# Cached values loaded 128 partitions wide, small buffers moved apart, attention scores over 64 partitions with the two heads of a pair side by side

## What is computed

```python
def _attend(q, k, v, mask, sinks):
    scores = jnp.einsum('...qkgd,...skd->...kgqs', q, k).astype(jnp.float32) * (HEAD_DIM ** -0.5)
    scores = jnp.where(mask, scores, NEG_INF)
    sink = jnp.broadcast_to(sinks.reshape(N_KV, GROUP, 1, 1).astype(jnp.float32), scores.shape[:-1] + (1,))
    probs = jax.nn.softmax(jnp.concatenate([scores, sink], axis=-1), axis=-1)[..., :-1]
    return jnp.einsum('...kgqs,...skd->...qkgd', probs.astype(v.dtype), v)
...
def sample_window_attention(q, k, v, sinks, k_buf, v_buf):
    B, T = q.shape[:2]
    kk = jnp.concatenate([k_buf.astype(k.dtype), k], axis=1)
    vv = jnp.concatenate([v_buf.astype(v.dtype), v], axis=1)
```

## Time and profile before

| what | value |
|---|---|
| device time, median of 3 runs | 1117.38 us |
| lowest and highest of the 3 | 1115.88 and 1118.61 us |
| span of the profiled execution | 1115.6 us |
| PE busy | 936.1 us (84%) |
| DVE busy | 403.5 us (36%) |
| ACT busy | 267.6 us (24%) |
| POOL busy | 120.9 us (11%) |
| moved by DMA | 268.84 MB, mean 241 GB/s |

### The profile page before, as it was taken

The page is one execution under the profiler, slowest core; times in us unless marked ns, Lnnn a source line. Parts: engine busy times, 40 slices in busy tenths (PEclk is TensorE's granted clock), DMA queues, the critical chain, the costliest instruction groups (busy, mean ns, idle before and its releaser), DMA issues.

```text
span 1115.6 us, 14382 instructions
## 1 busy us (share of the span) xinstructions
PE 936.1 (84%) x5619; PEld 631.1 (57%) x5619; DVE 403.5 (36%) x874; ACT 267.6 (24%) x508; POOL 120.9 (11%) x195
## 2 busy tenths in 40 slices
PE   7999952999999999999927998888887887887844
PEld 6999952888999998978823333322222222222311
DVE  4765831776564545265561111010110011001126
ACT  3556430444344342311110111100110011011111
POOL 3000401000000000000012122011111111110003
PEclk8999985999999999999957999999999999989986
DMA  9233440211122142723494899999999999999962
GB/s 290 76 77 76 127 96 21 75 42 52 62 77 76 55 135 77 195 100 137 176 416 179 336 422 420 422 421 424 422 422 421 423 424 423 420 422 423 422 243 112
DMA packets 87896, 268.84 MB, mean 241 GB/s; under 512 B 32657, under 2 KB 59405, under 8 KB 67330
## 3 DMA queue, kind: packets, MB, share of 16 engines
q1 hardware_dynamic: 77602, 254.89, 58.8%
q0 software_dynamic: 10240, 13.21, 3.6%
HBM read 263.17 MB, written 15.16 MB: 249 GB/s over the span
## 4 chain that ended last, share of the span: by engine, by line
PE 50%; DMA 27%; DVE 10%; SPq 4%; another core or an unknown queue 3%; ACT 3%; issue 2%; POOLq 0%; POOL 0%; DVEq 0%; ACTq 0%
DMA slot<-in_w_up 26%; PE ps L764 25%; PE ps L1066 7%; PE ps L1093 5%; PE ps L981 5%; SPq L459 4%; PE ps L851 2%; PE ps L805 1%; PE ps L885 1%; DVE rawL L1450 1%; PE ps L875 1%; DVE hL L1536 1%; PE ps L1049 1%; PE ps L1001 1%
## 5 line engine op out<-in xcount | busy, mean ns | idle before, releaser
L1066 PE MATMUL ps<-slot,xt 128*64 128x512 f32 x512 | 248.3, 634 | 71.5 <-DMA slot<-in_w_up 70.5
L1067 PE MATMUL ps<-slot,xt 128*64 128x512 f32 x512 | 248.6, 635 | 0.0
L1066 PEld LDWEIGHTS ps<-slot,xt 128*64 128x64 f32 x512 | 69.3, 144 | 222.1 <-issue 152.8
L764 PE MATMUL ps<-xTh,wh 128*128 128x260 f32 x704 | 149.4, 294 | 1.5 <-DVE rawL L1450 1.5
L764 PE MATMUL ps<-xTl,wh 128*128 128x260 f32 x704 | 144.0, 287 | 0.0
L764 PE MATMUL ps<-xTh,rawL 128*128 128x260 f32 x704 | 144.0, 286 | 0.0
L1928 DVE COPY xt<-ps 128x512 f32<-128x512 f32 x32 | 22.1, 692 | 295.8 <-PE ps L1049 295.8
L1093 PE MATMUL ps<-slot,hT 128*64 128x512 f32 x512 | 116.9, 598 | 1.4 <-DVE hT L1938 1.4
L764 PEld LDWEIGHTS ps<-xTh,wh 128*128 128x128 f32 x704 | 112.4, 194 | 2.8 <-issue 1.8
L764 PEld LDWEIGHTS ps<-xTl,wh 128*128 128x128 f32 x704 | 111.5, 194 | 0.0
L764 PEld LDWEIGHTS ps<-xTh,rawL 128*128 128x128 f32 x704 | 110.9, 193 | 0.0
(11 more groups left out here) (314 smaller groups left out, 1210.2 us busy)
## 6 DMA issues: line engine op xcount, KB each, us to landing
slot<-in_w_down SPq DMA_DIRECT2D x32, 2048.0 KB, 28.7
slot<-in_w_gate SPq DMA_DIRECT2D x64, 1024.0 KB, 27.8
slot<-in_w_up SPq DMA_DIRECT2D x64, 1024.0 KB, 32.4
raw<-in_w_in SPq DMA_DIRECT2D x18, 1024.0 KB, 5.1
raw<-in_w_in SPq DMA_DIRECT2D x16, 256.0 KB, 4.5
raw<-in_w_lru_out SPq DMA_DIRECT2D x4, 1024.0 KB, 5.1
raw<-in_w_attn_out SPq DMA_DIRECT2D x16, 256.0 KB, 4.6
wo_raw<-in_w_o SPq DMA_DIRECT2D x4, 1024.0 KB, 8.6
```

The lines of the kernel that those rows point to most:

```text
L764: last = mm(out_of[:, a, 0:HT], w[:, k, :], x[:, k, a * HT:(a + 1) * HT], start=(k == 0 and n == 0), stop=(k == KT - 1 and n == 2))
L1066: mm(out[0:CAP, :], tokens, w[:, q, :], start=start, stop=stop)
L1067: last = mm(out[CAP:P, :], tokens, w[:, 4 + q, :], start=start, stop=stop)
```

## The change

The zero-padded `kz` becomes `kT`, in which the two key heads of a pair lie in partitions 0 to 63 and 64 to 127 without zeros. A score product runs over 64 partitions. Half of a unit (`hh`) is now two query heads of each of the pair's two key heads, and the program alternates between the lower and the upper 64 partitions, with results in different PSUM banks. The softmax pieces `sk8` and `es` and the copies into `pT` are addressed to suit. ACT writes `kT` in one instruction instead of two, DVE copies the new key into `kS` in 2 instructions instead of 4, and POOL's two memsets go.

`cV` is loaded with all 128 partitions, and the new value is written over partition 0 afterwards by a DMA that waits for the load and is issued behind the nine outputs. `kwin` and `snew` move to the end of the region of `kT` and `vtok`, so the copies into `pT` no longer wait for them; SP waits for the outputs instead, before it loads `lnG` over that region.

```diff
@@ -163,8 +163,8 @@
...
-        kz = at("kz", [P, 2, 2, T], F32, oE)
-        vtok = at("vtok", [P, NB, 256], F32, oE + 4 * KB2)
+        kT = at("kT", [P, 2, T], F32, oE)
+        vtok = at("vtok", [P, NB, 256], F32, oE + 2 * KB2)
...
@@ -177,8 +177,8 @@
...
-        kwin = at("kwin", [P, 256], F32, oI + 12288)
-        snew = at("snew", [NS, 512], F32, oI + 13312)
+        kwin = at("kwin", [P, 256], F32, oE + 8288)
+        snew = at("snew", [NS, 512], F32, oE + 9312)
...
@@ -471,6 +471,7 @@
...
+            sp.wait_ge(s_kv_out, 64)
...
@@ -597,12 +598,6 @@
...
-            pool.wait_ge(s_cst, 6)
-            gp.memset(kz[0:HD, :, 1, :], 0.0).then_inc(s_cst, 1)
-            pool.wait_ge(s_cst, 7)
-            gp.memset(kz[HD:P, :, 0, :], 0.0).then_inc(s_cst, 1)
-            pool.wait_ge(s_cst, 8)
-
...
@@ -624,14 +619,15 @@
             pool.wait_ge(s_cv, 8)
             pool.wait_ge(s_ocT, 1)
             pool.dma_start(cK[:, :, :], A["cache_k"].rearrange("b w k d -> w b (k d)")).then_inc(s_ck, 16)
-            pool.dma_start(cV[1:P, :, :], A["cache_v"][:, 1:WIN, :, :].rearrange("b w k d -> w b (k d)")).then_inc(s_cv_ld, 16)
-
-            pool.dma_start(cV[0:1, :, :], snew[:, 256:512]).then_inc(s_cv_ld, 16)
+            pool.dma_start(cV[:, :, :], A["cache_v"].rearrange("b w k d -> w b (k d)")).then_inc(s_cv_ld, 16)
 
             pool.wait_ge(s_ocv, 2)
             pool.dma_start(O["conv_prompt"][0, :, :], oc[0:3, :]).then_inc(s_oc_out, 16)
             for b in range(NS):
                 pool.dma_start(O["conv_sample"][b, :, :], oc[4 + 4 * b:7 + 4 * b, :]).then_inc(s_oc_out, 16)
+
+            pool.wait_ge(s_cv_ld, 16)
+            pool.dma_start(cV[0:1, :, :], snew[:, 256:512]).then_inc(s_cv_ld, 16)
 
             pool.wait_ge(s_oc_out, 16 * 9)
             gp.memset(qz[:, :, :], 0.0).then_inc(s_qz, 1)
@@ -847,22 +843,24 @@
...
                 lo = 0 if n else P
-                for h in range(GRP):
-                    last = mm(pair[2][:, h // 2, (h % 2) * 256 + lo:(h % 2) * 256 + 256], qT[:, 4 * p2 + h, n * P:(n + 1) * P],
-                              kz[:, p2, par, (n - 1) * P + lo:(n + 1) * P], start=True, stop=True)
+                for h2 in range(2):
+                    for par in range(2):
+                        half = slice(par * HD, (par + 1) * HD)
+                        last = mm(pair[2][:, par, h2 * 256 + lo:h2 * 256 + 256], qT[half, 4 * p2 + 2 * hh + h2, n * P:(n + 1) * P],
+                                  kT[half, p2, (n - 1) * P + lo:(n + 1) * P], start=True, stop=True)
                 last.then_inc(s_sc, 1)
 
-            def probs_t(u, par):
+            def probs_t(u, hh):
                 p2, n = _UNITS[u]
...
@@ -901,7 +899,7 @@
...
-                pe.wait_ge(s_skd, 6)
+                pe.wait_ge(s_skd, 4)
...
@@ -1177,11 +1175,7 @@
                     sc.activation(xp[:, i, 3 + HT:3 + SEQ], ps[:, 1, 0:SEQ - HT], ACT.Identity, bias=bias)
                     sc.activation(xp[:, i, 3 + SEQ + 3:XPW:CONV], ps[:, 1, SEQ - HT:HT], ACT.Identity, bias=bias).then_inc(s_eva, 1)
                 elif kind == "k":
-                    if i == 0:
-                        act.wait_ge(s_cst, 8)
-                    for a in range(2):
-                        half = slice(a * HD, (a + 1) * HD)
-                        sc.activation(halves(kz[half, i, a, :]), both[half], ACT.Identity, bias=bias[half])
+                    sc.activation(halves(kT[:, i, :]), both, ACT.Identity, bias=bias)
                     lo = SEQ - P - HT
                     sc.activation(kl[:, i, :], ps[:, 1, lo:HT], ACT.Identity, bias=bias).then_inc(s_eva, 1)
                 elif kind == "v":
@@ -1245,27 +1239,28 @@
...
+                two = slice(2 * hh * P, (2 * hh + 2) * P)
...
-                    sc.activation(pT[:, par, 0, :], bank[6], ACT.Copy).then_inc(s_pa, 1)
+                    sc.activation(pT[:, :, 0, two], bank[6].rearrange("p (a q) -> p a q", a=2), ACT.Copy).then_inc(s_pa, 1)
...
-                    sc.activation(pT[:, par, 1, 0:256], bank[6][:, 0:256], ACT.Copy).then_inc(s_pa, 1)
+                    sc.activation(pT[:, 0, 1, two], bank[6][:, 0:256], ACT.Copy).then_inc(s_pa, 1)
...
@@ -1564,40 +1559,39 @@
...
-                    head = (2 * p2 + par) * GRP + h
...
+                    head = (2 * p2 + j // 2) * GRP + 2 * hh + j % 2
...
-                g = (2 * p2 + par) * GRP
-                v.tensor_tensor(es[:, par, :], sk8[:, g:g + GRP], mx[:, par, :], ALU.subtract).then_inc(s_nm, 1)
...
+                sk4 = sk8[:, 8 * p2:8 * p2 + 8].rearrange("p (a h) -> p a h", a=2)[:, :, 2 * hh:2 * hh + 2]
+                v.tensor_tensor(es[:, hh, :].rearrange("p (a h) -> p a h", a=2), sk4,
+                                mx[:, hh, :].rearrange("p (a h) -> p a h", a=2), ALU.subtract).then_inc(s_nm, 1)
...
-                link(v.tensor_tensor(dn[:, par, :], dn[:, par, :], es[:, par, :], ALU.add))
...
+                link(v.tensor_tensor(dn[:, hh, :], dn[:, hh, :], es[:, hh, :], ALU.add))
...
-                dve.wait_ge(s_tr, 2 * u + par + 1)
-                if u == 0:
-                    dve.wait_ge(s_kv_out, 64)
-                    dve.wait_ge(s_cv_ld, 32)
-                else:
+                dve.wait_ge(s_tr, 2 * u + hh + 1)
+                if u >= 1:
                     dve.wait_ge(s_pv, u)
                 if u == 1:
...
+                two = slice(2 * hh * P, (2 * hh + 2) * P)
...
-                    v.tensor_copy(pT[:, par, 1, :], bank[7]).then_inc(s_pd, 1)
+                    v.tensor_copy(pT[:, :, 1, two], bank[7].rearrange("p (a q) -> p a q", a=2)).then_inc(s_pd, 1)
...
-                    v.tensor_copy(pT[:, par, 1, 256:512], bank[7][:, 256:512]).then_inc(s_pd, 1)
+                    v.tensor_copy(pT[:, 1, 1, two], bank[7][:, 256:512]).then_inc(s_pd, 1)
...
@@ -1614,9 +1608,7 @@
...
-                        for a in range(2):
-                            half = slice(a * HD, (a + 1) * HD)
-                            v.tensor_copy(kS[half, p2, :, 0], kz[half, p2, a, SEQ:T]).then_inc(s_skd, 1)
+                        v.tensor_copy(kS[:, p2, :, 0], kT[:, p2, SEQ:T]).then_inc(s_skd, 1)
...
```

More of the change, by code:

```diff
@@ L833, in h_state, with scores @@
                 last.then_inc(s_ohT, 1)
-            def scores(u, par):
+            def scores(u, hh):
                 p2, n = _UNITS[u]
-                if par == 0:
+                if hh == 0:
                     if n == 0:
@@ L864, in probs_t @@
                     pe.wait_ge(s_spc, 1)
-                if u >= 1 and par == 0:
+                if u >= 1 and hh == 0:
                     pe.wait_ge(s_attl, u)
@@ L872, in probs_t @@
                         continue
-                    for h in range(GRP):
-                        to = 6 + (kt if n else h // 2)
-                        last = nc.tensor.transpose(bank[to][:, h * P:(h + 1) * P], sS[par][:, h, kt * P:(kt + 1) * P], ident[:, :])
+                    for j in range(GRP):
+                        to = 6 + (kt if n else j // 2)
+                        last = nc.tensor.transpose(bank[to][:, j * P:(j + 1) * P], sS[hh][:, j, kt * P:(kt + 1) * P], ident[:, :])
                 last.then_inc(s_tr, 1)
@@ L1246, in kv, with exps, probs_t @@
                 sc.activation(vtok[:, :, :].rearrange("p n c -> p (n c)"), flat[3], ACT.Copy).then_inc(s_kva, 1)
-            def exps(u, par):
+            def exps(u, hh):
                 p2, n = _UNITS[u]
                 lo = 0 if n else P
-                m = 2 * u + par
+                m = 2 * u + hh
                 act.wait_ge(s_nm, 2 * m + 2)
-                for h in range(GRP):
-                    sc.activation(sS[par][:, h, lo:256], sS[par][:, h, lo:256], ACT.Exp, bias=nm[:, par, h:h + 1],
-                                  accum_out=dn[:, par, h:h + 1]).then_inc(s_ex, 1)
-                sc.activation(es[:, par, :], es[:, par, :], ACT.Exp).then_inc(s_ex, 1)
-            def probs_t(u, par):
+                for j in range(GRP):
+                    sc.activation(sS[hh][:, j, lo:256], sS[hh][:, j, lo:256], ACT.Exp, bias=nm[:, hh, j:j + 1],
+                                  accum_out=dn[:, hh, j:j + 1]).then_inc(s_ex, 1)
+                sc.activation(es[:, hh, :], es[:, hh, :], ACT.Exp).then_inc(s_ex, 1)
+            def probs_t(u, hh):
                 p2, n = _UNITS[u]
-                act.wait_ge(s_tr, 2 * u + par + 1)
+                act.wait_ge(s_tr, 2 * u + hh + 1)
                 if u >= 1:
@@ L1553, in h_state, with masked @@
                     v.tensor_copy(oh[:, n * 512:(n + 1) * 512], pair[2][0:NS + 1, n, :]).then_inc(s_ohv, 1)
[L1555 removed]
+            def masked(u, hh):
                 p2, n = _UNITS[u]
                 lo = 0 if n else P
[L1559 removed]
+                m = 2 * u + hh
                 dve.wait_ge(s_sc, m + 1)
@@ L1566, in masked @@
                     dve.wait_ge(s_nrm, 4 * (m - 1))
-                for h in range(GRP):
-                    head = (2 * p2 + par) * GRP + h
```

(22 more changed lines are left out.)

12 lines of the change are left out of this document (5 added, 7 removed).

## The result

The changed kernel takes **1078.51 us** (median of 4 runs, 1077.19 to 1079.3), beside 1117.62 us for the kernel before (4 runs, 1115.88 to 1118.61): 39.1 us less, ratio 0.9653 (95% interval 0.964 to 0.9667). The forecast was 1073.8 us, with a range of 1069 to 1082. The profiled execution has a span of 1077.5 us, 38.1 less than before.

A forecast was written before the change was run, and what follows sets the result against it. Bounds: a stall on the cached-value load, then DVE and ACT, then PE from 270 to 420 us. Gains 36.2 + 7.0 + 0.4 = 43.6 us, so 1117.4 - 43.6 = 1073.8 us; range 1069 to 1082.

The forecast's parts named there:

- the likeliest case: Whole kernel: the change does as said, 1070 to 1077 us; chance 75%.
- The stall: DVE's first copies into pT no longer wait for cached values; PE's idle and low-clock time return, 36.2 us.
- the rival in which the stall only moves: Late rewrite of partition 0 makes sample_pv wait; slower than before, about 1119 at 105 us landing; chance 2%.
- The half chunk of `raw`: Weights ACT awaited 11.2 us within the stall: should land at 147, before ACT wants them; counted as nothing.
- The scores: Score groups in the PE-bound stretch: neighbours on different array halves overlap; ten long groups save 7.0 us.
- the group paid 0.14 besides: Score groups: 0.14 us mode-change cost per group, making a long group 1.03 us instead of 1.73.
- the floor I set by eight weight loads: Score groups: eight weight loads don't shrink with rows, so a group needs at least 0.87 to 0.89 us.
- `kS`, 0.4 us: New keys copied into kS in two copies instead of four, shortening PE's wait at L909: 0.4 us.
- The start: Memsets gone, cache copies start 1.9 us earlier; can push a first tile by no more than that; counted nothing.
- The expert loop "keeps its length": Expert loop: loads follow buffers PE frees, so it moves with what is ahead, length unchanged.
- the load stays on one engine: Cached-value load: 128 partitions don't spread; stall still goes, ACT waits for weights; 1077 to 1080 us; chance 5%.
- some 40 us of room: POOL's queue: qz is read just before 184, some 40 us after POOL has issued everything.

The follow-up runs named there:

- e3: Kernel before with only the new 128-partition load, moved buffers and waits; old scores, kz and memsets: 1080.27 us.
- e6: Changed kernel with kwin and snew back under pT and DVE's two waits back, load still of 128 partitions: 1079.01 us.
- e9: Kernel before with the 127-partition load of cached values split into 112 and 15, readers' count raised to 48: 1082.27 us.
- e8: Changed kernel with all four products of a score group on the lower 64 partitions (computation altered): 1088.39 us.
- e1: Changed kernel with POOL's two early memsets put back, over kT, with ACT's wait for them: 1074.91 us.
- e2: Changed kernel, memsets still out, with the two memory-to-memory cache copies moved behind the output of h: 1074.64 us.
- e5: Changed kernel with the cV load back to 127 partitions, buffers still apart: 1091.76 us.
- e4: Kernel before with only the new kT and scores, memsets on kT; load of 127 partitions, old buffers and waits: 1109.9 us.

## Why the prediction held, and where it was off

The time, 1078.51, is in the range, 4.7 us over the forecast; the mechanism was that of the likeliest case. By its steps:

- **The stall, 36.2 us: right.** 36.4 by the two traces. With 128 partitions the wait is gone (e3), the old waits then cost nothing (e6), and the old kernel needs only the split (e9). Tile 20 takes 5.73. The landing came at 122.98 + 10.7 = 133.7 where I had 137.4, and the new value was in by 137.6, long before its reader. The products of `sample_pv` start at 213.63, so the rival in which the stall only moves was 76 us off. I had put them at 201, three tiles behind the scores of the sample tokens; the trace of before already had them 26.7 us behind these (247.36 against 220.69), with two groups of scores and the transposes L916, which wait for DVE, between the tiles.
- **The half chunk of `raw`: right.** ACT waits 1.8 us in all for weights between 115 and 165 us; PE doesn't see it.
- **The scores, 7.0 us: mechanism right, size 5.84.** The group took 1.06 for the 1.03 forecast. What was mis-sized is the step "the group paid 0.14 besides": I priced the mode change once, on the way in, and it is paid again by whatever comes next, 0.17 to 0.23 us a tile behind each of 12 groups, 2.5 us in all. Two things I had at nothing gave part of it back. The groups behind a product with values went from 1.93 to 1.06, the 0.20 that they had paid more than the others being gone, so that half of the long groups win 0.87 and not 0.70; and the short groups fell from 0.89 and 1.09 to 0.65. Together: 20.28 us of groups before, 10 x 1.06 + 2 x 0.65 = 11.9 after, less some 2.5, is 5.9. The 0.65 also shows that the floor I set by eight weight loads (0.87 to 0.89) isn't one: a short group's eight loads take 0.52 us on PEld after, 0.97 before and 0.96 in e8, so the loads for the two halves overlap too. The Trainium skill, "TensorEngine Tiling (Array Packing)", section "Key Properties", says that a change of mode drains TensorE. The trace agrees in so far as a change has a price, about 0.2 us each way; the drain itself is in no row.
- **`kS`, 0.4 us: not seen.** PE's wait at L907 did fall from 1.74 to 1.06. But the same stretch gained 0.64 of waiting two places on, at L914 (2.62 to 3.26), and more time at the low clock: the sample products with values, L921, took 4.50 us at a granted clock of 0.80 where before they took 3.63 at 1.00. Net, this stretch lost 0.3. The prediction's rows had the waits at L909 and L875 and not the one of 2.62. I hadn't asked what a shift of a few us does to a stretch in which PE's clock goes up and down with its waits.
- **The start, "nothing": the step that failed.** The words were that the two copies "can push a first tile by no more than these 1.9 us, and the first weights have to wait for the transposes of x anyway". The bound was wrong: the copies moved up by 2.2 us, and the first tile came 3.2 us later. I had no reason to take the one for a bound of the other: each copy takes 10.4 to 11.4 us to land, and a load behind it could lose any part of that (this is argued, no run measured it). And the cover was the wrong one: behind the transposes of x PE waits for the small loads into `vec`, which I had not looked at. 2.8 us were still missing at 151.58, and e1 and e2 win back 3 to 4 (their ratios are 0.0027 and 0.0032 lower, and their medians 3.6 and 3.9 us).
- **The expert loop "keeps its length": about.** It was 2 us longer in this execution, 522.1 us from its first product to the end against 520.1, and the 1.0 us gained ahead of it went in there. The eleven kernels took between 519.1 (e5) and 522.4 us (e2). It may be more than scatter: the five that come to the loop first (at 550.8 to 556.3) took 521.0 to 522.4, the six that come later (558.1 to 595.5) 519.1 to 520.6. With one trace each this stays open.
- **The rival "the load stays on one engine", 1077 to 1080: its price was wrong.** e5 is that case, and costs 13 us and not 3 to 6. The wait that I followed, through the weights and DVE to unit 0's product with values, was forecast at some 3 us and came at 3.77. I left out what is queued on POOL: the memset of `qz` came at 200.27, and it is read, without the stall, at about 184. I had counted some 40 us of room for it in the likeliest case, and didn't ask what becomes of them when POOL is held.

The terms make 36.4 + 5.8 - 0.3 - 2.8 + 1.0 - 2.1 = 38.0 us, of the 38.1 by which the spans differ.

PE's time line after, for the step on `kS`:

```profile
186.37 1.08 PE L907 MATMUL ps<-kS,qz 128*32 128x128 f32 x32 [1.06 <-DVE qz L1618]
...
203.50 1.11 PE L914 MATMUL ps<-ident,sSm 128*128 128x128 f32 x4 [3.26 <-DVE sSm L1640]
...
213.63 4.50 PE L921 MATMUL ps<-pTs,cV 128*128 128x8 f32 x32
```

What stays open: how the 8 us of e5 that aren't the wait for `qz` split between its other two waits and the low clock, whether the expert loop's 2 us are scatter, and whether the small loads suffer from being behind the copies in order or from sharing the engines with them.

## What to carry to other kernels

Count the partitions of a large DMA before anything else: this load over 127 partitions ran at a share of 0.07 of the 16 engines, about one of them, and held everything behind it in its own queue, and loading one row too many and rewriting it, or splitting into 112 + 15, costs nearly nothing. Moving buffers so that fewer readers wait for such a load won about half of the stall (e4 against e5); making it fast won all of it. When an edit frees an engine early in the program, look at which transfers it now issues ahead of the small loads that everything starts from; "idle work" such as a memset may have been keeping an order that nothing else keeps. And a mode change on TensorE must be priced on both sides: in the group itself and in the group that comes next.

## What was not expected of the hardware

- One DMA of 1016 KB over 127 partitions landed after 64.0 us in e5, with 6.74 us of issue; 896 + 120 KB over 112 and 15 landed after 10.7, with 1.47 us of issue. While it ran, POOL's outputs of 12 KB were held for 52 to 56 us.
- Products over 64 partitions overlapped whatever their order (1.06 alternating, 1.07 in pairs), though no single one got shorter: the instructions of the line have a median of 376 ns after, 376 in e8 and 379 before. The gain is all in how their starts overlap.
- Two memory-to-memory copies of 1016 KB, issued 2.2 us earlier, made PE wait 4.82 us for loads of 1 to 16 KB that it had not waited for before, and its first tile start 3.2 us later.
